# A two-layer transformer with experts: a fourth buffer for split weights, kept rows fetched two at a time, and the last activation's low part ahead of the next expert's rows

## The chip, the cores and the metric

The kernel runs on one core of a Trainium2 chip, as one program. The metric is the device time of one execution in microseconds (us), lower is better. Three executions of the kernel before took 1961.27, 1962.09 and 1963.03 us; the median is 1962.09 us.

## The reference, cut to what matters

The program computes two blocks of two layers each in float32 (sequence 256, width 1024). The change lies in the mixture of experts, the feed-forward part of the first block's second layer:

```python
def swiglu(x, wg, wu, wd):
    return (jax.nn.silu(x @ wg) * (x @ wu)) @ wd

def moe_swiglu(xn, router, wg, wu, wd):       # 8 experts, top 2, inner width 3584
    t = xn.reshape(B * S, D)                  # 256 tokens x 1024
    logits = (t @ router).astype(jnp.float32)
    top_val, top_idx = lax.top_k(logits, TOP_K)
    gates = jax.nn.softmax(top_val, axis=-1)
    combine = jnp.sum(jax.nn.one_hot(top_idx, N_EXPERTS) * gates[..., None], axis=1)
    out = jnp.zeros_like(t)
    for e in range(N_EXPERTS):
        out = out + combine[:, e:e + 1] * swiglu(t, wg[e], wu[e], wd[e])
    return out
```

Before it stand attention, retention and a dense feed-forward part, behind it a gated embedding and the whole second block; the change leaves those as they are.

## The kernel before

**Pieces and products.** All weights stream from HBM in pieces of 128x2048 float32 (1 MB) into seven slots of the tile `raw`. Products keep float32 precision by splitting: for each piece ScalarE (ACT) writes a rounded copy, the high part (`high<-raw`, L1630 in the experts), and VectorE (DVE) writes the rest, the low part (`low<-raw,high`, L2555). TensorE (PE) then multiplies high by high, high by low and low by high (L726, L727, L728). There are `PARTS` = 3 buffers for the two parts; piece k uses buffer k % 3.

**An expert.** The tokens of an expert (at most 128) are gathered as rows, turned, scaled and split into `xg_hi` (ACT, L1637, eight instructions) and `xg_lo` (DVE, L2538, eight). An expert has 42 pieces, numbered by `EXPERT_ORDER`: for j = 0 to 6 two gate pieces, two up pieces and, from j = 1 on, the two down pieces of j - 1; the two down pieces of j = 6 come last. So gate 3 is pieces 16 and 17, up 3 is 18 and 19, down 2 is 20 and 21; up 6 is 36 and 37, down 5 is 38 and 39, down 6 is 40 and 41. Each piece is 12 matmuls of 512 columns. After gate j (and for j = 6 after piece 38) PE turns the hidden activation of the group before (`turn_hidden`, L1149); ACT copies it as `hT_hi` (L1645), DVE makes `hT_lo` (L2566), and the first matmul of that group's down waits for `hT_lo`.

**What sets the order.** No scheduler is at work: each engine's instructions stand in the order in which the code writes them, with waits on semaphores between engines. `expert` exists once for each of the three engines. On ACT and DVE it walks over the 42 pieces; at step q (piece q has been used by PE) it splits piece q + 3, and where q is the second gate piece of a group it then handles the activation: ACT runs `copy(j - 1)` and the silu (L1661), DVE runs `low_hidden(j - 1)`. At the second up piece DVE first multiplies (L2575) and then splits. At up 6's second piece (q = 37) DVE also runs `gathered` for the next expert; at q = 38 it runs `low_hidden(6)`, before the split of that step. Experts 1 to 6 are a loop, expert 0 and expert 7 are written out. In expert 0 DVE also works out where each token's kept rows lie (`kept_places`, after the split of q = 19).

**Kept rows.** Experts 0 to 6 store their outputs to HBM from `scr` (`expert_traffic` on GpSimd, POOL). In expert 7 POOL fetches each token's rows by four indirect DMAs of 128 rows into the tile `kept` (L1941), which lies over `xT_hi` and `xT_lo`, the tiles of the input activations, idle during the experts. DVE adds them to `h` at q = 13, 19, 25 and 31 (`add_kept`, L2649).

Of the kernel before, what the change touches and what calls it, by code (L numbers as in the profile page):

```python
# [76 lines left out]
EXPERT_ORDER = expert_order()  # L77

# [54 lines left out]
def program(nc, io, out, cut=99):  # L133
    ctx = ExitStack()
    with ctx:
# [102 lines left out]
        kept = sb("kept", [P, 2 * NT, D], over="xT_hi")  # L238
# [57 lines left out]
        moe_sems[1].update(turns=14, by_dma=False)  # L296
        moe_sems[0].update(high=high_done, low=low_done, used=pieces_used, landed=landed, ring=(0, RAW))
# [387 lines left out]
        def _(pe):  # L685
# [413 lines left out]
            def expert(e, s, first, is_first, is_last):  # L1099
# [7 lines left out]
                def product(what, j):  # L1107
                    for half in range(2):
# [14 lines left out]
                        if what == "down":  # L1123
                            w = [x[:, k % PARTS, :].rearrange("p (k n) -> p k n", k=2) for x in (high, low)]
                            columns_first = is_last and (j, half) == (GROUPS - 1, 1)
                            for n in range(4):
                                f, c = (n % 2, n // 2) if columns_first else (n // 2, n % 2)
                                ff = 2 * half + f
                                last = exact(bank[4 + c][:, :], [x[:, j % 2, ff * P:(ff + 1) * P] for x in (hT_hi, hT_lo)],
                                             [x[:, f, c * CHUNK:(c + 1) * CHUNK] for x in w],  # L1130
                                             j == 0 and ff == 0, j == GROUPS - 1 and ff == 3)
                                if columns_first and n == 1:
                                    last.then_inc(s["half"], 1)
                        else:
                            w = [x[:, k % PARTS, :].rearrange("p (k n) -> p k n", k=4) for x in (high, low)]
# [281 lines left out]
        def _(act):  # L1417
# [206 lines left out]
            def expert_split(e, s, first, loads0, k):  # L1624
# [16 lines left out]
            def expert(e, s, first, loads0, is_first, is_last, again=False):  # L1641
# [5 lines left out]
                for q, (what, j, half) in enumerate(EXPERT_ORDER):  # L1647
# [34 lines left out]
            def finish(s, first):  # L1682

                if s["by_dma"]:
                    act.wait_ge(outputs_stored, 16 * N_EXPERTS)
# [21 lines left out]
            def all_experts(s, first, loads0, again):  # L1707
                for k in range(0 if again else 1, PARTS):
                    expert_split(0, s, first, loads0, k)
# [128 lines left out]
            for l in range(LAYERS):  # L1838
# [12 lines left out]
                if l == 1:  # L1851
                    expert_split(0, moe_sems[0], moe_first, moe_landed, 0)
# [65 lines left out]
        def _(pool):  # L1918
# [6 lines left out]
            def expert_traffic(s):  # L1925
# [24 lines left out]
        def _(dve):  # L1950
# [601 lines left out]
            def expert_split(e, s, first, k):  # L2552
                at0, slots = s["ring"]
                dve.wait_ge(s["high"], first + PER_EXPERT * e + k + 1)
                dve.tensor_tensor(low[:, k % PARTS, :], raw[:, at0 + k % slots, :], high[:, k % PARTS, :].bitcast(F32),  # L2555
                                  ALU.subtract).then_inc(s["low"], 1)

            def expert(e, s, first, first_slot, is_first, is_last, again=False):
# [10 lines left out]
                for q, (what, j, half) in enumerate(EXPERT_ORDER):  # L2569
# [7 lines left out]
                    if q + PARTS < PER_EXPERT:  # L2577
                        expert_split(e, s, first, q + PARTS)
                    elif not is_last:
                        expert_split(e + 1, s, first, q + PARTS - PER_EXPERT)  # L2580
                    elif not again and q + PARTS < PER_EXPERT + AHEAD:
# [61 lines left out]
            def add_kept(n):  # L2643

                t = n % NT
                dve.wait_ge(kept_in, 16 * 2 * NT)
                if n >= NT:
                    dve.wait_ge(kept_added, n - NT + 1)
                dve.scalar_tensor_tensor(out=h[:, t, :], in0=kept[:, n, :], scalar=kept_gate[:, n:n + 1],  # L2649
                                         in1=h[:, t, :], op0=ALU.mult, op1=ALU.add).then_inc(kept_added, 1)  # L2650

            def finish(s):

                for c in range(2):
                    y_low(s, N_EXPERTS - 1, c).then_inc(s["ylow"], 1)
                if s["by_dma"]:
                    dve.wait_ge(kept_added, 2 * NT)
# [276 lines left out]
```

## Time and profile before

| what | value |
|---|---|
| median of 3 executions | 1962.09 us |
| profiled execution's own time | 1963.61 us |
| its span, first to last instruction | 1961.8 us |
| PE busy (matmuls) | 1915.7 us, 98% |
| DVE busy | 1516.9 us, 77% |
| ACT busy | 1227.8 us, 63% |
| HBM read | 507.56 MB, mean 262 GB/s |
| expert outputs stored | first at 641.8 us, last at 1364.1 us |

The page names the busy time of each engine, the groups of instructions and who waited for whom. The waits are read first, then the timeline of each engine around the places where PE waited; start times are in us from the span's start. A matmul row's duration (0.39 us) is longer than the distance to the next one, since matmuls overlap: PE's pace is read from the starts. A store of an expert's outputs follows the end of that expert; six experts lie between the first and the last, 120.4 us each.

### The profile page before, as it was taken

To read this page: it belongs to the slowest core of one execution; us is meant where nothing else is said; L and a number is where in the kernel's file an instruction comes from. 1 tells how busy PE (TensorE), PEld (TensorE's weight loads), DVE (VectorE), ACT (ScalarE), POOL (GpSimd) and SP (SyncE) were. 2 spreads that over 40 slices of the span, in tenths; PEclk is the share of its full clock that TensorE was granted. 3 is DMA by queue.
4 is the path that set the end of the run, shared out by engine and by line. 5 is a ranking of instruction groups with operands and counts; after the bars stand their busy time and mean duration, and the time that the engine had idled before them with its cause. 6 is when DMAs were issued, how large, how long until landed. Compare 5 with 4: busy or idle time off the path is not lost.

```text
span 1961.8 us, 26828 instructions
## 1 busy us (share of the span) xinstructions
PE 1915.7 (98%) x10275; PEld 1627.7 (83%) x10275; DVE 1516.9 (77%) x1478; ACT 1227.8 (63%) x1332; POOL 29.8 (2%) x28
## 2 busy tenths in 40 slices
PE   8999999999899999999999999999999999999998
PEld 7879998888688888888888888888887788888987
DVE  5675555656798888888888888888997865877586
ACT  4554535555677777777777777777777546354542
POOL 0000000000000000000000000000100000000000
PEclk9999999999999999999999999999999999999999
DMA  7717555431799999999999999999996452345321
GB/s 250 250 47 259 189 177 171 151 129 70 282 373 355 392 371 376 386 352 392 377 364 384 358 385 384 365 381 357 396 378 226 163 168 97 123 159 193 129 94 37
DMA packets 246211, 514.62 MB, mean 262 GB/s; under 512 B 12516, under 2 KB 59240, under 8 KB 246120
## 3 DMA queue, kind: packets, MB, share of 16 engines
q1 hardware_dynamic: 242936, 502.77, 71.0%
q0 software_dynamic: 2896, 10.49, 1.3%
q8 instruction: 62, 1.02, 0.2%
q14 instruction: 29, 0.24, 0.0%
q10 hardware_dynamic: 288, 0.11, 0.0%
HBM read 507.56 MB, written 5.77 MB: 262 GB/s over the span
## 4 chain that ended last, share of the span: by engine, by line
PE 80%; DVE 11%; ACT 4%; issue 2%; SPq 2%; DMA 1%; DVEq 0%; ACTq 0%
PE bank L726 25%; PE bank L728 24%; PE bank L727 24%; DVE low L1958 3%; DVE low L2555 1%; ACT high L1630 1%; PE bank L697 1%; PE bank L1149 1%; PE bank L850 1%; ACT high L1427 1%; SPq L636 1%; SPq L675 1%; DVE xg_lo L2538 1%; DVE at L2765 1%; PE bank L841 1%
## 5 line engine op out<-in xcount | busy, mean ns | idle before, releaser
L2555 DVE TENSOR_TENSOR low<-raw,high 128x2048 fp32r<-128x2048 f32 x336 | 767.7, 2290 | 110.5 <-ACT high L1630 109.8
L1630 ACT ACTIVATE high<-raw 128x2048 fp32r<-128x2048 f32 x336 | 644.4, 1922 | 244.4 <-PE bank L728 243.0
L1958 DVE TENSOR_TENSOR low<-raw,high 128x2048 fp32r<-128x2048 f32 (+1 forms) x138 | 310.4, 2259 | 162.7 <-ACT high L1427 162.3
L1427 ACT ACTIVATE high<-raw 128x2048 fp32r<-128x2048 f32 (+1 forms) x138 | 260.6, 1894 | 164.7 <-PE bank L728 152.2
L726 PE MATMUL bank<-high,xg_hi 128*128 128x512 f32 x896 | 353.8, 395 | 1.5 <-DVE xg_lo L2538 1.0
L728 PE MATMUL bank<-high,xg_lo 128*128 128x512 f32 x896 | 349.5, 390 | 0.0
L727 PE MATMUL bank<-low,xg_hi 128*128 128x512 f32 x896 | 348.9, 389 | 0.0
L726 PE MATMUL bank<-high,xT_hi 128*128 128x512 f32 (+1 forms) x576 | 227.3, 395 | 3.1 <-DVE xT_lo L1980 1.3
L728 PE MATMUL bank<-high,xT_lo 128*128 128x512 f32 (+1 forms) x576 | 221.5, 385 | 0.0
L727 PE MATMUL bank<-low,xT_hi 128*128 128x512 f32 (+1 forms) x576 | 221.0, 384 | 0.0
L726 PE MATMUL bank<-high,hT_hi 128*128 128x512 f32 x536 | 210.3, 392 | 8.3 <-DVE hT_lo L2566 8.3
L727 PE MATMUL bank<-low,hT_hi 128*128 128x512 f32 x536 | 208.8, 390 | 0.0
L728 PE MATMUL bank<-high,hT_lo 128*128 128x512 f32 x536 | 208.7, 389 | 0.0
L726 PEld LDWEIGHTS bank<-high,xg_hi 128*128 128x128 f32 x896 | 168.3, 188 | 36.3 <-issue 1.3
L728 PEld LDWEIGHTS bank<-high,xg_lo 128*128 128x128 f32 x896 | 168.1, 188 | 35.8
L727 PEld LDWEIGHTS bank<-low,xg_hi 128*128 128x128 f32 x896 | 168.5, 188 | 33.5
L726 PE MATMUL bank<-xT_hi,high 128*128 128x256 f32 x672 | 192.4, 286 | 3.4 <-issue 1.8
L727 PE MATMUL bank<-xT_lo,high 128*128 128x256 f32 x672 | 190.9, 284 | 0.0
L728 PE MATMUL bank<-xT_hi,low 128*128 128x256 f32 x672 | 190.8, 284 | 0.0
L726 PEld LDWEIGHTS bank<-xT_hi,high 128*128 128x128 f32 x672 | 129.6, 193 | 4.7 <-issue 2.0
L727 PEld LDWEIGHTS bank<-xT_lo,high 128*128 128x128 f32 x672 | 129.6, 193 | 0.4
L728 PEld LDWEIGHTS bank<-xT_hi,low 128*128 128x128 f32 x672 | 129.6, 193 | 0.0
(346 smaller groups left out, 2208.8 us busy)
## 6 DMA issues: line engine op xcount, KB each, us to landing
raw<-in_moe_w_gate SPq DMA_DIRECT2D x112, 1024.0 KB, 6.9
raw<-in_moe_w_up SPq DMA_DIRECT2D x112, 1024.0 KB, 7.1
raw<-in_moe_w_down SPq DMA_DIRECT2D x112, 1024.0 KB, 7.0
raw<-in_w_in SPq DMA_DIRECT2D x63, 1024.0 KB, 5.1
raw<-in_w_out SPq DMA_DIRECT2D x20, 1024.0 KB, 4.8
raw<-in_dense_w_gate SPq DMA_DIRECT2D x11, 1024.0 KB, 5.2
raw<-in_dense_w_up SPq DMA_DIRECT2D x11, 1024.0 KB, 5.2
raw<-in_dense_w_down SPq DMA_DIRECT2D x11, 1024.0 KB, 4.8
```

The costliest lines, as they stand in the source:

```text
L636: sp.dma_start(dst, src).then_inc(landed[slot], 16)
L675: sp.dma_start(dst, source).then_inc(consts_in, 16)
L697: last = pe.transpose(bank_of(key)[:, (k * NT + t) * P:(k * NT + t + 1) * P], rows[:, t, (2 * j + k) * P:(2 * j + k + 1) * P], ident[:, :])
L726: pe.matmul(dst, stationary[0], moving[0], start=start, stop=False)
L727: pe.matmul(dst, stationary[0], moving[1], start=False, stop=False)
L728: return pe.matmul(dst, stationary[1], moving[0], start=False, stop=stop)
L841: last = pe.transpose(bank[2 + g % 2][:, b * P:(b + 1) * P], probs[:, g % 2, b * P:(b + 1) * P], ident[:, :])
L850: last = pe.matmul(att_out(name, u, t), probsT[:, g % 2, c0 + s * P:c0 + (s + 1) * P], val[:, s, :], start=(s == 0), stop=(s == n // P - 1))
L1427: act.activation(high[:, slot, 0:k * n], raw[:, raw_slot[piece], 0:k * n], ACT.Copy).then_inc(high_done, 1)
L1630: act.activation(high[:, k % PARTS, :], raw[:, slot, :], ACT.Copy).then_inc(s["high"], 1)
L1958: dve.tensor_tensor(low[:, slot, 0:k * n], src, high[:, slot, 0:k * n].bitcast(F32), ALU.subtract).then_inc(low_done, 1)
L2555: dve.tensor_tensor(low[:, k % PARTS, :], raw[:, at0 + k % slots, :], high[:, k % PARTS, :].bitcast(F32), ALU.subtract).then_inc(s["low"], 1)
```

## The change

Four things change.

1. In the experts' main pass split weights get a fourth buffer, `high3` over `xT_hi` and `low3` over `xT_lo`. `expert_parts(4)` gives buffers k % 4 to pieces 0 to 11, three buffers (0, 1, 2) in turn to pieces 12 to 17, and four again to pieces 18 to 41, so that each expert begins at buffer 0. Its list `ahead[q]` says which pieces are split at step q: mostly piece q + 4; at q = 11 none; at q = 12 to 16 piece q + 3; at q = 17 pieces 20 and 21; from q = 18 on piece q + 4 again.
2. `kept` moves to the two tiles `a2` and `scr`: POOL fetches two blocks of rows, and each of the other two only when DVE has added the block that lay in its place.
3. DVE runs `gathered` for the next expert at q = 38, behind `low_hidden(6)`, instead of at q = 37, ahead of it.
4. `finish` waits for the added rows before it reuses `scr` and `a2`.

```diff
+def expert_parts(slots):
+    three = 6 if slots == 4 else len(EXPERT_ORDER)
+    start = 12 if slots == 4 else 0
+    slot = [k % 4 if k < start else ((k - start) % 3 if k < start + three else (k - start - three) % 4)
+            for k in range(len(EXPERT_ORDER))]
+    n = len(slot)
+    prev = [max(i for i in range(-n, k) if slot[i % n] == slot[k]) for k in range(n)]
+    ahead, at = [[] for _ in range(n)], slots
+    for q in range(n):
+        while at < n + slots and (prev[at] if at < n else prev[at - n] + n) <= q:
+            ahead[q].append(at)
+            at += 1
+    return slot, prev, ahead
...
-        kept = sb("kept", [P, 2 * NT, D], over="xT_hi")
+        kept = (a2, scr)
+        high3 = sb("high3", [P, HALF], F32R, over="xT_hi")
+        low3 = sb("low3", [P, HALF], F32R, over="xT_lo")
...
 (ACT, expert_split)
-                act.wait_ge(s["used"], first + PER_EXPERT * e + k - PARTS + 1)
-                act.activation(high[:, k % PARTS, :], raw[:, slot, :], ACT.Copy).then_inc(s["high"], 1)
+                act.wait_ge(s["used"], first + PER_EXPERT * e + s["part_before"][k] + 1 + (s["by_dma"] and is_first and k < PARTS))
+                act.activation(expert_part(s, k)[0], raw[:, slot, :], ACT.Copy).then_inc(s["high"], 1)
...
 (ACT, expert; DVE the same)
-                    if q + PARTS < PER_EXPERT:
-                        expert_split(e, s, first, loads0, q + PARTS)
-                    elif not is_last:
-                        expert_split(e + 1, s, first, loads0, q + PARTS - PER_EXPERT)
-                    elif not again and q + PARTS < PER_EXPERT + AHEAD:
+                    for k in ([PARTS] if is_first and q == 0 and s["by_dma"] else []) + s["parts_ahead"][q]:
+                        if k < PER_EXPERT:
+                            expert_split(e, s, first, loads0, k)
+                        elif not is_last:
+                            expert_split(e + 1, s, first, loads0, k - PER_EXPERT)
+                    if is_last and not again and PER_EXPERT <= q + PARTS < PER_EXPERT + AHEAD:
                         split(moe_first + N_EXPERTS * PER_EXPERT + q + PARTS - PER_EXPERT)
...
 (POOL, expert_traffic)
+                pool.wait_ge(rows_turned, 2 * (N_EXPERTS - 1))
                 pool.wait_ge(outputs_stored, 16 * N_EXPERTS)
                 for n in range(2 * NT):
-                    pool.indirect_dma_start(kept[:, n, :], None, expert_rows,
+                    if n >= 2:
+                        pool.wait_ge(kept_added, n - 1)
+                    pool.indirect_dma_start(kept[n % 2][:, :], None, expert_rows,
...
 (DVE, expert)
+                    if (what, j, half) == ("down", GROUPS - 2, 0) and not is_last and s["by_dma"]:
+                        gathered(rows_high, 2 * e, rows_low, (1, 3))
...
-                    if (what, j, half) == ("up", GROUPS - 1, 1) and not is_last:
-                        if s["by_dma"]:
-                            gathered(rows_high, 2 * e, rows_low, (1, 3))
-                        else:
-                            gathered(s["thigh"], 9 * e + 8, s["tfree"], (7, 6))
+                    if (what, j, half) == ("up", GROUPS - 1, 1) and not is_last and not s["by_dma"]:
+                        gathered(s["thigh"], 9 * e + 8, s["tfree"], (7, 6))
...
 (DVE, add_kept)
-                dve.wait_ge(kept_in, 16 * 2 * NT)
+                dve.wait_ge(kept_in, 16 * 2 * (n // 2 + 1))
```

**First place: DVE in expert 0 around gate 3.** The rows run from the end of up 2 (the product into `v_63` on bank2) to the same product of up 3 (bank3). Before, five splits (pieces 16 to 20) stand between that product and `hT_lo` of group 2:

```order
L2575 TENSOR_TENSOR v_63<-v_63,bank2 128x512 [waits pieces_used,moe0_silu]
L2555 TENSOR_TENSOR low_51<-raw_49,high_50 128x2048 [waits high_parts_done] x5
L2566 TENSOR_TENSOR hT_lo_111<-bank7,hT_hi_110 128x512 [waits moe0_thigh]
L2555 TENSOR_TENSOR low_51<-raw_49,high_50 128x2048 [waits high_parts_done]
L2575 TENSOR_TENSOR v_63<-v_63,bank3 128x512 [waits pieces_used,moe0_silu]
```

After the change, in the same stretch (`low3` is the low half of the fourth buffer):

```order
L2609 TENSOR_TENSOR v_63<-v_63,bank2 128x512 [waits pieces_used,moe0_silu]
L2589 TENSOR_TENSOR low_51<-raw_49,high_50 128x2048 [waits high_parts_done] x5
L2589 TENSOR_TENSOR low3_116<-raw_49,high3_115 128x2048 [waits high_parts_done]
L2600 TENSOR_TENSOR hT_lo_111<-bank7,hT_hi_110 128x512 [waits moe0_thigh]
L2589 TENSOR_TENSOR low_51<-raw_49,high_50 128x2048 [waits high_parts_done]
L2609 TENSOR_TENSOR v_63<-v_63,bank3 128x512 [waits pieces_used,moe0_silu]
```

Six splits (16 to 21) now stand there: step 17 splits pieces 20 and 21, both ahead of `hT_lo` of group 2. On ACT both high parts likewise stand ahead of `hT_hi` of that group.

**Second place: DVE at the end of expert 0.** The rows run from the last multiplication (up 6, into `v_63`) to the last split of the expert's code. Before:

```order
L2575 TENSOR_TENSOR v_63<-v_63,bank2 128x512 [waits pieces_used,moe0_silu]
L2555 TENSOR_TENSOR low_51<-raw_49,high_50 128x2048 [waits high_parts_done]
L2538 SCALAR_TENSOR_TENSOR xg_lo_107<-bank1,gcols_74,xg_hi_106 128x128 [waits taken_rows_high]
L2538 SCALAR_TENSOR_TENSOR xg_lo_107<-bank1,gcols_74,xg_hi_106 128x128 x3
L2538 SCALAR_TENSOR_TENSOR xg_lo_107<-bank3,gcols_74,xg_hi_106 128x128 [waits taken_rows_high]
L2538 SCALAR_TENSOR_TENSOR xg_lo_107<-bank3,gcols_74,xg_hi_106 128x128 x3
L2566 TENSOR_TENSOR hT_lo_111<-bank7,hT_hi_110 128x512 [waits moe0_thigh]
L2555 TENSOR_TENSOR low_51<-raw_49,high_50 128x2048 [waits high_parts_done] x4
```

After:

```order
L2609 TENSOR_TENSOR v_63<-v_63,bank2 128x512 [waits pieces_used,moe0_silu]
L2589 TENSOR_TENSOR low3_116<-raw_49,high3_115 128x2048 [waits high_parts_done]
L2600 TENSOR_TENSOR hT_lo_111<-bank7,hT_hi_110 128x512 [waits moe0_thigh]
L2571 SCALAR_TENSOR_TENSOR xg_lo_107<-bank1,gcols_74,xg_hi_106 128x128 [waits taken_rows_high]
L2571 SCALAR_TENSOR_TENSOR xg_lo_107<-bank1,gcols_74,xg_hi_106 128x128 x3
L2571 SCALAR_TENSOR_TENSOR xg_lo_107<-bank3,gcols_74,xg_hi_106 128x128 [waits taken_rows_high]
L2571 SCALAR_TENSOR_TENSOR xg_lo_107<-bank3,gcols_74,xg_hi_106 128x128 x3
L2589 TENSOR_TENSOR low_51<-raw_49,high_50 128x2048 [waits high_parts_done] x3
L2589 TENSOR_TENSOR low3_116<-raw_49,high3_115 128x2048 [waits high_parts_done]
```

`hT_lo` of group 6 now stands ahead of the eight `xg_lo`, and the split ahead of it is that of piece 41 instead of piece 40.

## Rows read from the trace of the kernel before

**Rows 1.** The page: busy us, share of the span, instructions.
```profile
PE 1915.7 (98%) x10275; PEld 1627.7 (83%) x10275; DVE 1516.9 (77%) x1478; ACT 1227.8 (63%) x1332; POOL 29.8 (2%) x28
```

**Rows 2.** Waits of PE over the span: us in total, times, longest.
```profile
PE bank L726 <- DVE hT_lo L2566: 8.3, 7, 1.3
...
PE bank L726 <- DVE low L2555: 0.4, 1, 0.4
```

**Rows 3.** Timeline of PE, expert 1, piece 39 to 40: start, us, instruction.
```profile
751.57 0.39 PE L728 MATMUL bank<-high,hT_lo 128*128 128x512 f32 x1
753.12 0.50 PE L726 MATMUL bank<-high,hT_hi 128*128 128x512 f32 x1 [1.17 <-DVE hT_lo L2566]
753.46 0.40 PE L727 MATMUL bank<-low,hT_hi 128*128 128x512 f32 x1
```

**Rows 4.** Timeline of ACT, end of expert 1.
```profile
746.08 1.92 ACT L1630 ACTIVATE high<-raw 128x2048 fp32r<-128x2048 f32 x1 [0.80 <-PE bank L728]
747.91 2.15 ACT L1637 ACTIVATE xg_hi<-bank,gcols 128x128 fp32r<-128x128 f32 x8
749.90 0.65 ACT L1645 ACTIVATE hT_hi<-bank 128x512 fp32r<-128x512 f32 x1
```

**Rows 5.** Timeline of DVE, end of expert 1.
```profile
747.52 0.68 DVE L2575 TENSOR_TENSOR v<-v,bank 128x512 f32<-128x512 f32 x1
748.12 2.28 DVE L2555 TENSOR_TENSOR low<-raw,high 128x2048 fp32r<-128x2048 f32 x1
750.32 2.15 DVE L2538 SCALAR_TENSOR_TENSOR xg_lo<-bank,gcols,xg_hi 128x128 fp32r<-128x128 f32 x8
752.39 0.68 DVE L2566 TENSOR_TENSOR hT_lo<-bank,hT_hi 128x512 fp32r<-128x512 f32 x1
```

**Rows 6.** Timeline of PE, expert 0, piece 39 to 40.
```profile
631.03 0.39 PE L728 MATMUL bank<-high,hT_lo 128*128 128x512 f32 x1
632.74 0.47 PE L726 MATMUL bank<-high,hT_hi 128*128 128x512 f32 x1 [1.32 <-DVE hT_lo L2566]
633.04 0.40 PE L727 MATMUL bank<-low,hT_hi 128*128 128x512 f32 x1
```

**Rows 7.** Timeline of PE, expert 0, before piece 23.
```profile
581.25 0.39 PE L728 MATMUL bank<-high,xg_lo 128*128 128x512 f32 x1
582.07 0.50 PE L726 MATMUL bank<-high,xg_hi 128*128 128x512 f32 x1 [0.43 <-DVE low L2555]
```

**Rows 8.** Timeline of PE, expert 0, before piece 5.
```profile
529.28 0.39 PE L728 MATMUL bank<-high,xg_lo 128*128 128x512 f32 x1
529.62 0.50 PE L726 MATMUL bank<-high,xg_hi 128*128 128x512 f32 x1
```

**Rows 9.** Timeline of ACT, expert 2, step 17 (gate 3).
```profile
809.27 1.92 ACT L1630 ACTIVATE high<-raw 128x2048 fp32r<-128x2048 f32 x1 [0.80 <-PE bank L728]
811.10 0.57 ACT L1645 ACTIVATE hT_hi<-bank 128x512 fp32r<-128x512 f32 x1
```

**Rows 10.** Timeline of DVE, expert 2, step 17 (gate 3).
```profile
811.22 2.29 DVE L2555 TENSOR_TENSOR low<-raw,high 128x2048 fp32r<-128x2048 f32 x1 [0.43 <-ACT high L1630]
813.43 0.68 DVE L2566 TENSOR_TENSOR hT_lo<-bank,hT_hi 128x512 fp32r<-128x512 f32 x1
```

**Rows 11.** Timeline of PE, expert 2, last matmuls of piece 19, first of 20.
```profile
812.04 0.39 PE L728 MATMUL bank<-high,xg_lo 128*128 128x512 f32 x1
...
814.76 0.39 PE L728 MATMUL bank<-high,xg_lo 128*128 128x512 f32 x1
814.98 0.39 PE L726 MATMUL bank<-high,hT_hi 128*128 128x512 f32 x1
```

**Rows 12.** Timeline of DVE, expert 7: second and third block added.
```profile
1421.69 1.28 DVE L2649 SCALAR_TENSOR_TENSOR h<-kept,kept_gate,h 128x1024 f32<-128x1024 f32 x1
...
1438.53 1.28 DVE L2649 SCALAR_TENSOR_TENSOR h<-kept,kept_gate,h 128x1024 f32<-128x1024 f32 x1
```

**Rows 13.** The tile `kept`: its four fetches, issue to landing.
```profile
DMA to landing us min/median/max: 8.5/9.1/10.1
```

More of the change, by code:

```diff
@@ L237, in program, with expert_part @@
         taken_rows = a2
-        kept = sb("kept", [P, 2 * NT, D], over="xT_hi")
+        kept = (a2, scr)
+        high3 = sb("high3", [P, HALF], F32R, over="xT_hi")
+        low3 = sb("low3", [P, HALF], F32R, over="xT_lo")
+        def expert_part(s, k):
+            slot = s["part"][k]
+            return (high[:, slot, :], low[:, slot, :]) if slot < PARTS else (high3[:, :], low3[:, :])
         logit_rows = yf[0:N_EXPERTS, NT * D:NT * D + SEQ]
@@ L296, in program @@
         moe_sems[1].update(turns=14, by_dma=False)
+        for s, slots in zip(moe_sems, (PARTS + 1, PARTS)):
+            s["part"], s["part_before"], s["parts_ahead"] = expert_parts(slots)
         moe_sems[0].update(high=high_done, low=low_done, used=pieces_used, landed=landed, ring=(0, RAW))
@@ L1123, in product @@
                         if what == "down":
-                            w = [x[:, k % PARTS, :].rearrange("p (k n) -> p k n", k=2) for x in (high, low)]
+                            w = [x.rearrange("p (k n) -> p k n", k=2) for x in expert_part(s, k)]
                             columns_first = is_last and (j, half) == (GROUPS - 1, 1)
@@ L1134, in product @@
                         else:
-                            w = [x[:, k % PARTS, :].rearrange("p (k n) -> p k n", k=4) for x in (high, low)]
+                            w = [x.rearrange("p (k n) -> p k n", k=4) for x in expert_part(s, k)]
                             dst = bank[(0 if what == "gate" else 2) + j % 2]
@@ L1622, in attention2, with expert_split @@
                 splits(pieces_of["ih", l][1])
-            def expert_split(e, s, first, loads0, k):
+            def expert_split(e, s, first, loads0, k, is_first=False):
                 at0, slots = s["ring"]
@@ L1708, in all_experts @@
                 for k in range(0 if again else 1, PARTS):
-                    expert_split(0, s, first, loads0, k)
+                    expert_split(0, s, first, loads0, k, True)
                 gathered(s["tfull"], 1, s["thigh"], (6, 7))
@@ L2554, in expert_split @@
                 dve.wait_ge(s["high"], first + PER_EXPERT * e + k + 1)
-                dve.tensor_tensor(low[:, k % PARTS, :], raw[:, at0 + k % slots, :], high[:, k % PARTS, :].bitcast(F32),
+                high_part, low_part = expert_part(s, k)
+                dve.tensor_tensor(low_part, raw[:, at0 + k % slots, :], high_part.bitcast(F32),
                                   ALU.subtract).then_inc(s["low"], 1)
@@ L2576, in expert @@
                                           ALU.mult).then_inc(s["hm"], 1)
[L2577 to L2581, printed above, removed]
+                    if (what, j, half) == ("down", GROUPS - 2, 0) and not is_last and s["by_dma"]:
+                        gathered(rows_high, 2 * e, rows_low, (1, 3))
+                    for k in ([PARTS] if is_first and q == 0 and s["by_dma"] else []) + s["parts_ahead"][q]:
+                        if k < PER_EXPERT:
+                            expert_split(e, s, first, k)
+                        elif not is_last:
+                            expert_split(e + 1, s, first, k - PER_EXPERT)
+                    if is_last and not again and PER_EXPERT <= q + PARTS < PER_EXPERT + AHEAD:
                         split(moe_first + N_EXPERTS * PER_EXPERT + q + PARTS - PER_EXPERT)
@@ L2645, in add_kept @@
                 t = n % NT
[L2646 removed]
+                dve.wait_ge(kept_in, 16 * 2 * (n // 2 + 1))
                 if n >= NT:
                     dve.wait_ge(kept_added, n - NT + 1)
[L2649 removed]
+                dve.scalar_tensor_tensor(out=h[:, t, :], in0=kept[n % 2][:, :], scalar=kept_gate[:, n:n + 1],
                                          in1=h[:, t, :], op0=ALU.mult, op1=ALU.add).then_inc(kept_added, 1)
             def finish(s):
+                if s["by_dma"]:
+                    dve.wait_ge(kept_added, 2 * NT)
                 for c in range(2):
                     y_low(s, N_EXPERTS - 1, c).then_inc(s["ylow"], 1)
[L2656 to L2657 removed]
                 for n in range(4):
```

4 lines of the change are left out of this document (2 added, 2 removed).

## The prediction

> **What bounds the kernel now.** I read the busy shares first: PE is busy for 1915.7 of 1961.8 us [rows 1]. So a gain can only come from PE's own waits, and DVE and ACT matter only where PE waits for one of their results. The list of waits comes next. Of those that the change can touch, one is large: PE waits seven times for `hT_lo`, 8.3 us in all, the longest 1.3; for a low part (`low` L2555) it waits once, 0.4 us [rows 2]. Then the timeline of PE shows where: between piece 39 and piece 40 of an expert, once in each of experts 0 to 6 (expert 7 gathers nothing for a next one). PE's undisturbed pace is read from starts: twelve matmuls from 812.04 to 814.76, so 0.227 us each and 2.72 us a piece [rows 11].
>
> A wait costs more than its idle time. In expert 1 the matmul behind 751.57 starts at 753.12: 1.55 us instead of 0.227, so 1.32 lost; the one after it starts 0.34 later instead of 0.227, 0.11 more: 1.43 us [rows 3]. In expert 0: 1.71 less 0.227 is 1.48, then 0.30 instead of 0.227: 1.55 us [rows 6]. Less the largest, the other six have (8.3 - 1.3) / 6 = 1.17 us of idle each, the same as in rows 3, so they repeat. Seven waits cost 1.55 + 6 x 1.43 = 10.1 us. Two small ones in expert 0 are for low parts that come late: before piece 23 0.82 - 0.227 = 0.59, and with the slow restart of rows 3 0.70 us [rows 7]; before piece 5 0.34 - 0.227 = 0.11, with restart 0.22 us [rows 8].
>
> **End of an expert: DVE reordered, one more buffer.** Take expert 1. PE's end of piece 37 releases ACT at 746.08 [rows 4]. That step now splits piece 41 instead of 40; its duration and trigger are those of the row. ACT then makes `xg_hi` from 747.91 and `hT_hi` from 749.90 to 750.55, as before. DVE multiplies at 747.52 and splits from 748.12 to 750.40 [rows 5]. Before, the eight `xg_lo` (2.15 us) stood next and `hT_lo` ended at 753.07. Now `hT_lo` is next, waits for 750.55 and ends at about 751.26. PE wants it at 751.57 + 0.23 = 751.80, so it is there 0.54 us early. The `xg_lo` then end at about 753.4 and the low part of the next expert's piece 0 at about 755.6 (2.2 us after). PE wants both two pieces later, at 751.80 + 5.44 = 757.24: 1.6 us of cover. Each half of the change alone would not do: with three buffers piece 41's low part would follow the `xg_lo` and end at about 755.6 against a need at 754.5. All seven waits go, -10.1 us.
>
> The fourth buffer gives every other split outside the three-buffer stretch one piece, 2.72 us, more lead than its trigger gives it now. The lateness of 0.59 and 0.11 us in expert 0 is less than that: -0.9 us. If it stays after all, this term is 0.
>
> **Step 17: two splits ahead of one activation.** This is what speaks against the change. The return from three buffers to four needs one step that splits two pieces, and it is step 17, the second gate piece of group 3, which also carries the activation of group 2. The order shows six splits instead of five ahead of that `hT_lo`. In expert 2 the stretch now reads: ACT splits from 809.27 and copies `hT_hi` from 811.10 [rows 9]; DVE splits from 811.22 and makes `hT_lo` from 813.43, so it ends at 814.11 [rows 10]; PE wants it at 814.98 [rows 11]. Cover: 0.87 us. After the change ACT splits piece 20 at 809.27, piece 21 one step later (1.83 us, from rows 9) at 811.10 to 813.02, and copies `hT_hi` at 812.93 to 813.5. DVE splits piece 20 at 811.22, piece 21 at 811.22 + 2.20 (the step from 748.12 to 750.32 in rows 5) = 813.42, and `hT_lo` runs 2.21 later (rows 10), at 815.63 to 816.31. PE starts 0.05 behind (753.07 to 753.12 in rows 3 and 5), at 816.36 instead of 814.98: 1.38 us, with the restart 1.49. Nothing hides it: piece 20 is the first to read that activation, and PE has no other work in its program in between. The landing of piece 21's weights is not in question, since its split is asked for only one step early.
>
> It happens in all eight experts, since all run with four buffers: 8 x 1.49 = +11.9 us. No row shows two splits ahead of a small copy at this place, so I bound it: 0.87 us of cover against one DVE split of 2.20 to 2.29 gives 1.33 to 1.42; with a restart of 0.07 to 0.11 that is 1.4 to 1.5, and if ACT or DVE fall a further 0.2 behind, 1.7; if something I do not see lets DVE begin 0.3 us sooner, 1.1. So +8.8 to +13.6, and I take 11.9. Behind it DVE and ACT are one piece ahead, and piece 22 onward has its low part in time.
>
> The engine's order is what this term hangs on. In the trace DVE did not take `hT_lo` ahead of the `xg_lo` written before it, although its input was there at 750.55 and it ran at 752.39 [rows 4, 5]. The Trainium skill (Perfetto Trace Analysis, Tensor Engine Instruction) says that ScalarE, VectorE and GpSimd queues are strict FIFO and only TensorE's has a limited reorder, for weight loads; by that rule the term stands, by an engine that picked the ready instruction it would be 0. The trace agrees with the rule.
>
> **Kept rows in pairs.** The third and fourth fetch start only after an add. The fourth may start when the second add is over, 1421.69 + 1.28 = 1422.97 [rows 12]; the longest of four landings took 10.1 us [rows 13], so by 1433.1. The third add, which waits for that pair, stands at 1438.53 [rows 12]. Cover: 5.4 us, and PE another 2.7 behind DVE's. The queue holds nothing else then. Cost 0; were a landing 10 us later than any seen, +2 us. The first pair is fetched as now: the added wait, for rows turned in expert 6, is over by then. In `finish` the changed wait is for adds that ended 20 us before.
>
> **New tiles.** Splits into `low3` and `high3` have the same shape. No row shows them; for a duration as of the nearest rows, 0; a few per cent either way would vanish in the lead of 2.7 us.
>
> **The sum.** -10.1 - 0.9 + 11.9 = +0.9 us. The span goes from 1961.8 to 1962.7, the profiled execution's own time from 1963.61 to 1964.5. The three timed runs lie 1.5 us lower than that execution, at a median of 1962.09: predicted 1962.9 us. I call within 0.2% (3.9 us: 1958.2 to 1966.0) no change; it is about what a measurement of this kernel can tell.
>
> **The rivals.**
> - *The second split at step 17 hides.* Only the end-of-expert waits and the two small ones go: 1962.1 - 11.0 = 1951.1 us. For it: DVE idles before most splits, 0.43 us in rows 10, and the step before (q = 11 without a split) leaves it free. Against it: that idle lies before the first of the two splits, which still waits for PE's release; and 2.2 us is more than the cover of 0.87. 0.11.
> - *The end-of-expert wait stays, and the new one comes on top: slower.* Place: `hT_lo` of group 6. It holds only if it ends before 751.80, and its input comes from ACT at 750.55, behind `xg_hi`. If ACT's part slides by more than 0.54 us, the wait is back in part; if it slides by 1.8 us, all of it. Price: 10.1 us not saved, so -0.9 + 11.9 = +11.0, 1973.1 us. For it: the cover is the thinnest of all. Against it: ACT's four instructions and their triggers are unchanged in kind and count. 0.07.
> - *The fetch of kept rows comes too late*: +2 us at 10 us late, inside my range. 0.03.
>
> **How the numbers follow.** The forecast has 0.79. Its own bounds are -11.0 or -10.1, with +8.8 to +13.6: -2.2 to +3.5, so 1959.9 to 1965.6 us. The range reaches a little to both sides for a wait half removed or half as long, 1958.5 to 1967.0; that leaves out the fast and the slow rival, 0.18. Faster 0.12 (the fast rival and a little), same 0.78, slower 0.10 (the slow rival, and a new wait longer than bounded).
>
> **What would show it.** The changed profile should have no PE wait for `hT_lo` between pieces 39 and 40, and eight between pieces 19 and 20, each about 1.2 us of idle, 120 us apart; the total of waits for `hT_lo` would go from 8.3 to about 10. No PE wait for a low part in the experts. Outputs stored 120.4 us apart, as now. The fourth fetch lands before 1434 and the third add follows its split without a gap. I am wrong if the wait at piece 20 is missing or under 0.5 us, or if waits at piece 40 remain.

## The result, and the profile after

| | before | changed |
|---|---|---|
| median of 8 runs, us | 1962.12 (1961.27 to 1963.11) | 1967.79 (1966.16 to 1972.19) |
| profiled execution, us (its span) | 1963.61 (1961.8) | 1967.32 (1965.5) |

The ratio is 1.0023 with the 95% interval 1.0014 to 1.0031. On the 1962.09 us of the start that is 1966.6 us; the forecast was 1962.9 in a range that ends at 1967.0. So the change costs 2.7 to 6.1 us where no change was forecast. The middle of that interval, 4.5 us, is above the 3.9 us that I called no change, and its lower end is below. The same kernel measured once more (experiment 10) gave 1.0026 (1.0015 to 1.0037), so the loss is real and about 4.5 to 5 us.

The page, to be read beside [rows 1]: PE's work is unchanged, the span is 3.7 us longer.

```profile
span 1965.5 us, 26840 instructions
...
PE 1916.3 (97%) x10275; PEld 1629.0 (83%) x10275; DVE 1515.1 (77%) x1478; ACT 1226.1 (62%) x1332; POOL 31.0 (2%) x28
```

The lines of the changed kernel are numbered some 30 higher: L755 to L757 are the old L726 to L728, the low split is L2589, `hT_lo` L2600, `xg_lo` L2571, `select`'s probabilities L2558, the kept add L2683. The waits of PE in the experts (us in total, times, longest), beside [rows 2]:

```profile
PE bank L755 <- DVE hT_lo L2600: 10.1, 8, 1.4
...
PE bank L755 <- DVE xg_lo L2571: 2.1, 1, 2.1
...
PE bank L1196 <- DVE probs L2558: 1.7, 1, 1.7
```

The wait for a low part in the experts is gone. `hT_lo` has eight waits where it had seven, and they are at another place. The wait for `xg_lo` stands ahead of expert 0's first piece and was 1.0 us; it is taken up with the sum below. End of expert 1, DVE, beside [rows 5] (start, us, instruction, in brackets the idle time ahead of it and what ended it):

```profile
751.43 2.29 DVE L2589 TENSOR_TENSOR low<-raw,high 128x2048 fp32r<-128x2048 f32 x1
753.90 0.69 DVE L2600 TENSOR_TENSOR hT_lo<-bank,hT_hi 128x512 fp32r<-128x512 f32 x1 [0.18 <-ACT hT_hi L1674]
754.51 2.15 DVE L2571 SCALAR_TENSOR_TENSOR xg_lo<-bank,gcols,xg_hi 128x128 fp32r<-128x128 f32 x8
```

and PE at the same place, beside [rows 3]:

```profile
754.89 0.39 PE L757 MATMUL bank<-high,hT_lo 128*128 128x512 f32 x1
755.11 0.39 PE L755 MATMUL bank<-high,hT_hi 128*128 128x512 f32 x1
```

`hT_lo` ends at 754.59 and piece 40 begins at 755.11 without a gap: 0.52 us of cover, 0.54 predicted. Step 17 in expert 2, first ACT, then DVE, then PE, beside [rows 9 to 11]:

```profile
811.13 3.72 ACT L1659 ACTIVATE high<-raw 128x2048 fp32r<-128x2048 f32 x2 [0.80 <-PE bank L757]
814.76 0.58 ACT L1674 ACTIVATE hT_hi<-bank 128x512 fp32r<-128x512 f32 x1
```

```profile
813.09 4.49 DVE L2589 TENSOR_TENSOR low<-raw,high 128x2048 fp32r<-128x2048 f32 x2 [0.43 <-ACT high L1659]
817.50 0.68 DVE L2600 TENSOR_TENSOR hT_lo<-bank,hT_hi 128x512 fp32r<-128x512 f32 x1
```

```profile
816.62 0.39 PE L757 MATMUL bank<-high,xg_lo 128*128 128x512 f32 x1
818.24 0.50 PE L755 MATMUL bank<-high,hT_hi 128*128 128x512 f32 x1 [1.23 <-DVE hT_lo L2600]
818.57 0.39 PE L756 MATMUL bank<-low,hT_hi 128*128 128x512 f32 x1
```

`hT_hi` was ready at 815.34, and DVE was busy with the second low split until 817.58. PE starts 1.62 us after 816.62 instead of 0.227, so 1.39 lost, and the next matmul 0.33 later instead of 0.227: 1.50 us. It stands in all eight experts (575.57, 696.15, 816.62 and so on to 1419.20). In the first and the last of them the step from start to start is 1.77 us, so these two cost 1.62 us each and the eight together 12.2.

What the forecast did not have is in expert 0, at the token matmul behind piece 5. PE of the kernel before:

```profile
532.26 0.39 PE L728 MATMUL bank<-high,xg_lo 128*128 128x512 f32 x1
533.32 0.58 PE L1167 MATMUL bank<-a,probs 128*128 128x1 f32 x4 [0.67 <-DVE probs L2525]
...
534.46 0.39 PE L727 MATMUL bank<-low,xg_hi 128*128 128x512 f32 x1
534.69 0.40 PE L728 MATMUL bank<-high,xg_lo 128*128 128x512 f32 x1
```

and of the changed kernel:

```profile
532.16 0.39 PE L757 MATMUL bank<-high,xg_lo 128*128 128x512 f32 x1
534.24 0.58 PE L1196 MATMUL bank<-a,probs 128*128 128x1 f32 x4 [1.69 <-DVE probs L2558]
...
536.57 0.63 PE L756 MATMUL bank<-low,xg_hi 128*128 128x512 f32 x1
537.00 0.63 PE L757 MATMUL bank<-high,xg_lo 128*128 128x512 f32 x1
```

From start to start the gap is 2.08 us instead of 1.06, so 1.0 more. Behind it the matmuls of piece 6 start 0.43 us apart instead of 0.23. The stretches by window (us, busy time of PE, PEld, DVE, ACT and POOL, granted clock, DMA share, GB/s), before and after:

```profile
533.00:540.00 7.00, 6.68 (x34) 5.70 (x35) 6.20 (x7) 4.57 (x5) 1.04 (x1) 1.00 1.02 361
```

```profile
533.00:540.00 7.00, 5.76 (x23) 4.78 (x24) 6.26 (x10) 2.91 (x4) 0.41 (x1) 0.76 0.99 363
```

In this stretch the granted clock, 1.00 (2.4 GHz) before, was at 0.5 (1.2 GHz) for 3.4 us from 535.5 on. Piece 6 took 4.40 us instead of 2.85: 1.55 us more. Why `probs` comes later is seen on DVE. Before:

```profile
530.09 2.28 DVE L2555 TENSOR_TENSOR low<-raw,high 128x2048 fp32r<-128x2048 f32 x1
532.29 0.16 DVE L2522 COPY ssum<-routing 128x2 f32<-128x2 f32 x1
```

After:

```profile
520.87 6.70 DVE L2589 TENSOR_TENSOR low<-raw,high 128x2048 fp32r<-128x2048 f32 x3 [2.80 <-ACT high L1659]
...
531.00 2.29 DVE L2589 TENSOR_TENSOR low<-raw,high 128x2048 fp32r<-128x2048 f32 x1
533.21 0.16 DVE L2555 COPY ssum<-routing 128x2 f32<-128x2 f32 x1
```

With a fourth buffer expert 0 splits four pieces instead of three ahead. That extra split stands ahead of `select` (the picking of the next expert's tokens, at step 3), and `select` starts 0.92 us later.

The sum over the experts, as differences of PE's gaps: -10.2 (seven waits) - 0.9 (before pieces 23 and 5, both gone) + 12.2 (eight waits) + 1.0 (token matmul) + 1.6 (half clock) = +3.7 us. It is to be held against the experts alone, from the first matmul of expert 0 to the last one of expert 7 that reads `hT_lo`. Before:

```profile
508.19 6.48 PE L1222 MATMUL bank<-probs,yf 128*128 128x128 f32 x32 [0.65 <-DVE probs L2525]
...
515.81 0.47 PE L726 MATMUL bank<-high,xg_hi 128*128 128x512 f32 x1 [1.03 <-DVE xg_lo L2538]
...
1478.80 0.39 PE L728 MATMUL bank<-high,hT_lo 128*128 128x512 f32 x1
```

After:

```profile
508.59 5.23 PE L1251 MATMUL bank<-probs,yf 128*128 128x128 f32 x32 [0.87 <-DVE probs L2558]
...
515.98 0.47 PE L755 MATMUL bank<-high,xg_hi 128*128 128x512 f32 x1 [2.06 <-DVE xg_lo L2571]
...
1482.61 0.39 PE L757 MATMUL bank<-high,hT_lo 128*128 128x512 f32 x1
```

That is 962.99 us before and 966.63 after, +3.64. PE waits 1.0 us longer for `xg_lo` here, but the 32 small matmuls ahead of it took 1.25 us less, and expert 0 starts only 0.17 us later. That the whole spans also differ by 3.7 us is therefore partly chance. In the second profile of the changed kernel (experiment 10) the experts take 966.58 us, the same, but they start at 513.20 and the span is 1962.0 us, hardly more than before.

### The profile page after: what moved, and what is told of

It is laid out like the page before. It is cut to its first block, busy times and chain, and to the rows that moved or that the text cites. A ratio compares the mean times of both kernels' runs of the same rounds, so it can differ in the third digit from the quotient of the medians.

```text
span 1965.5 us, 26840 instructions
## 1 busy us (share of the span) xinstructions
PE 1916.3 (97%) x10275; PEld 1629.0 (83%) x10275; DVE 1515.1 (77%) x1478; ACT 1226.1 (62%) x1332; POOL 31.0 (2%) x28
## 4 chain that ended last, share of the span: by engine, by line
PE 83%; DVE 9%; ACT 4%; issue 3%; DMA 0%; ACTq 0%; DVEq 0%
PE bank L755 26%; PE bank L757 25%; PE bank L756 25%; DVE low L1991 3%; PE bank L726 1%; ACT high L1659 1%; PE bank L1178 1%; ACT high L1456 1%; PE bank L879 1%; DVE low L2589 1%; DVE at L2799 1%; PE bank L870 1%; PE bank L848 1%; DVE kT L2824 0%; DVE qT L2823 0%
## 5 line engine op out<-in xcount | busy, mean ns | idle before, releaser
L2589 DVE TENSOR_TENSOR low<-raw,high 128x2048 fp32r<-128x2048 f32 x336 | 765.5, 2290 | 110.9 <-ACT high L1659 109.3
L755 PE MATMUL bank<-high,xg_hi 128*128 128x512 f32 x896 | 354.0, 395 | 2.1 <-DVE xg_lo L2571 2.1
L757 PE MATMUL bank<-high,xg_lo 128*128 128x512 f32 x896 | 350.1, 391 | 0.0
L755 PE MATMUL bank<-high,xT_hi 128*128 128x512 f32 (+1 forms) x576 | 227.2, 394 | 3.4 <-DVE xT_lo L2013 1.3
L757 PE MATMUL bank<-high,xT_lo 128*128 128x512 f32 (+1 forms) x576 | 221.4, 384 | 0.0
L755 PE MATMUL bank<-high,hT_hi 128*128 128x512 f32 x536 | 210.4, 392 | 10.1 <-DVE hT_lo L2600 10.1
L757 PE MATMUL bank<-high,hT_lo 128*128 128x512 f32 x536 | 208.7, 389 | 0.0
L755 PEld LDWEIGHTS bank<-high,xg_hi 128*128 128x128 f32 x896 | 168.7, 188 | 35.9 <-issue 2.3
L757 PEld LDWEIGHTS bank<-high,xg_lo 128*128 128x128 f32 x896 | 168.5, 188 | 35.9
L755 PE MATMUL bank<-xT_hi,high 128*128 128x256 f32 x672 | 193.0, 287 | 3.7 <-issue 2.1
L757 PE MATMUL bank<-xT_hi,low 128*128 128x256 f32 x672 | 191.2, 284 | 0.0
L755 PEld LDWEIGHTS bank<-xT_hi,high 128*128 128x128 f32 x672 | 130.1, 194 | 5.2 <-issue 2.4
L757 PEld LDWEIGHTS bank<-xT_hi,low 128*128 128x128 f32 x672 | 130.1, 194 | 0.0
```

Of the source, the lines that this page charges most:

```text
L755: pe.matmul(dst, stationary[0], moving[0], start=start, stop=False)
L757: return pe.matmul(dst, stationary[1], moving[0], start=False, stop=stop)
L2589: dve.tensor_tensor(low_part, raw[:, at0 + k % slots, :], high_part.bitcast(F32), ALU.subtract).then_inc(s["low"], 1)
```

## The experiments

Each is a variant of the changed kernel. Ratios are to the kernel before, run beside it on the same chip, with their 95% intervals. Before had a median of 1963.54 us beside the first four, 1963.32 beside the next four and 1961.91 beside the last two. Where a stretch of the experts is given, it runs between the two matmuls named above. My theory: the double step at 17 costs 12 us, the lead in expert 0 ahead of `select` some 2.6 to 4, and all the rest is free. The rivals: the kept rows in pairs or the new buffers themselves cost something; the 1.0023 is scatter.

**1. The double step later.** One number moves the three-buffer stretch to pieces 20 to 25 and the double step from 17 to 25.

```diff
-    start = 12 if slots == 4 else 0
+    start = 20 if slots == 4 else 0
```

> Only the place of the three-buffer stretch moves: pieces 20 to 25 instead of 12 to 17, so that the step that splits two pieces is 25 (second piece of up 4), where no activation is copied. My theory (two splits ahead of one activation): the eight PE waits for hT_lo between pieces 19 and 20 go, 8 x 1.5 = 12 us, no others come, and the time is 1967.8 - 12 = about 1956 us, 0.3% below the kernel before. Rival (any step with two splits costs the same, wherever it stands): eight waits of 1.4 us move to pieces 26 or 28 and the time stays at 1967 to 1968. Rival (the loss is in memory or clock, not in this wait): under 3 us of change.

Measured: 1954.0 us (1952.28 to 1954.66), ratio 0.9953 (0.9939 to 0.9966). The list of waits:

```profile
PE bank L1196 <- DVE probs L2558: 1.8, 1, 1.8
PE bank L755 <- DVE xg_lo L2571: 1.1, 1, 1.1
PE bank L755 <- DVE hT_lo L2600: 0.6, 1, 0.6
```

Fifteen of the waits in question are gone, old and new; one of 0.6 us is left, in expert 7, where four splits stand between a kept add and that `hT_lo`. The place of the double step is the difference between loss and gain: 0.70% or 14 us against the changed kernel. In the profiles the experts take 953.54 us instead of 966.63, 13.1 less: 12.2 for the eight waits and 1.6 because the clock does not fall behind the token wait, less 1.0 for that last wait and a slightly longer token wait, make 12.8.

**2. `select` ahead of step 3's splits.** It stood behind them.

```diff
+                    if (what, j, half) == ("up", 0, 1) and not is_last and s["by_dma"]:
+                        select(e + 1, s, first_slot, e + 1)
...
-                    if (what, j, half) == ("up", 0 if s["by_dma"] else 2, 1) and not is_last:
+                    if (what, j, half) == ("up", 2, 1) and not is_last and not s["by_dma"]:
```

> DVE picks the next expert's tokens (select, four small instructions) ahead of the split of step 3 instead of behind it; all else as in the changed kernel. My theory for what the forecast left out: in expert 0 the extra early split pushes select back by 0.93 us, PE's wait at piece 6 grows from 0.83 to 1.85 us, and the clock that falls behind it costs another 1.6 us. Then this wait goes in expert 0 (the pick is done 2.2 us earlier), the eight matmuls at half clock go, and the time falls by 1.85 + 1.6 = 3.5 us plus 6 x 0.2, to about 1963; the scatter of the runs (6 us) falls to that of the kernel before (2 us). Rival (the clock falls there by chance, whatever PE did): the wait goes but some stretch at half clock stays in or near expert 0, and the scatter stays at 6 us; about 1965.5.

Measured: 1964.51 us (1961.09 to 1966.28), ratio 1.0004 (0.9995 to 1.0013). DVE now has `probs` before the splits, and `hT_lo` behind them:

```profile
530.09 0.48 DVE L2558 TENSOR_SCALAR probs<-a,ssum 128x128 f32<-128x128 f32 x2
...
530.69 6.70 DVE L2589 TENSOR_TENSOR low<-raw,high 128x2048 fp32r<-128x2048 f32 x3
...
537.37 0.68 DVE L2600 TENSOR_TENSOR hT_lo<-bank,hT_hi 128x512 fp32r<-128x512 f32 x1
```

The token matmul no longer waits and the clock is not lowered behind it, but a ninth wait for `hT_lo` appears (0.6 us idle, 0.8 lost, at 537; list: 10.8 us, 9 times). The experts take 963.70 us, 2.9 less than in the changed kernel; by the ratios it is 0.19 to 0.22% off the changed kernel's 1.0023 and 1.0026, some 4 us. The expected smaller scatter did not come: the runs lie 5 us apart, and those of the kernel before lie 8 us apart on this chip.

**3. Both.** The two edits above together.

```diff
-    start = 12 if slots == 4 else 0
+    start = 20 if slots == 4 else 0
...
+                        select(e + 1, s, first_slot, e + 1)
```

> The two edits before together: double step at 25, select ahead of the split. My theory: both savings add, 1967.8 - 12 - 4.7 = about 1951 us. Rival (one wait hides the other's saving): above 1954.

Measured: 1953.08 us (1951.76 to 1954.28), ratio 0.9950 (0.9937 to 0.9964). The waits:

```profile
PE bank L755 <- DVE hT_lo L2600: 1.2, 2, 0.6
```

This lies between the 1951 us of the expectation and the 1954 of its rival. It is 0.03% better than the first and not 0.2%: within the intervals the second edit adds little here. In the profiles the experts take 952.12 us instead of 953.54, 1.4 less: the token wait (2.0 us) goes and a wait for `hT_lo` at piece 8 comes (0.8 us lost). The first's profile already had no lowered clock behind its token wait, so in it there was less to gain; that is a reading of one execution each, not a proof.

**4. The second split of step 17 behind the activation.** The places in the buffers stay, only the order in the step changes, on ACT and DVE alike.

```diff
-                    for k in (...) + s["parts_ahead"][q]:
+                    for k in (...) + (s["parts_ahead"][q][:1] if q == 17 else s["parts_ahead"][q]):
...
+                        for k in s["parts_ahead"][q][1:] if q == 17 else ():
+                            expert_split(e, s, first, k)
```

> Step 17 stays the double step, but ACT and DVE split piece 21 behind the activation of group 2 instead of ahead of it. My theory: hT_lo then ends at the same point as in the kernel before, all eight waits at piece 20 go, 1967.8 - 12 = about 1956 us, the same as with the stretch moved. Rival (two splits in a step are too much work for DVE at that place, in whatever order): the wait turns up at piece 21 or 22 as a late low part and half or more of the 12 us stays.

Measured: 1957.2 us (1952.96 to 1959.83), ratio 0.9966 (0.9953 to 0.9979). DVE in expert 2, where `hT_lo` follows one split:

```profile
809.06 2.29 DVE L2591 TENSOR_TENSOR low<-raw,high 128x2048 fp32r<-128x2048 f32 x1 [0.43 <-ACT high L1659]
811.27 0.68 DVE L2602 TENSOR_TENSOR hT_lo<-bank,hT_hi 128x512 fp32r<-128x512 f32 x1
811.87 4.48 DVE L2591 TENSOR_TENSOR low<-raw,high 128x2048 fp32r<-128x2048 f32 x2
```

The eight waits at piece 20 go with the order alone: it was the place in DVE's program, not the buffers. Three shorter waits are left elsewhere (1.5 us), and the token matmul waits 2.4 us with a half clock behind it. The last of the three follows an add of kept rows for which DVE waited, in this experiment alone:

```profile
1431.46 1.28 DVE L2687 SCALAR_TENSOR_TENSOR h<-a,kept_gate,h 128x1024 f32<-128x1024 f32 x1 [1.83 <-DMA scr<-expert_rows,kept_row]
```

So the kept rows in pairs are free in the changed kernel and not in each variant of it; the last section comes back to this.

**5. The lead built later.** Expert 0 keeps three pieces of lead to step 3 and takes its fourth at step 4, behind `select`.

```diff
+                    early = is_first and s["by_dma"]
-                    for k in (...) + s["parts_ahead"][q]:
+                    for k in [q + 3] if early and q < 4 else ([7, 8] if early and q == 4 else s["parts_ahead"][q]):
```

> As the changed kernel, but expert 0 keeps three pieces of lead up to step 3 and gains the fourth at step 4, behind select: the extra split no longer stands ahead of select. My theory (the extra split delays select and with it PE at piece 6): the wait at piece 6 is back at 0.8 us as in the kernel before, 1.0 us less than in the changed one, and the clock behind it falls less often; ratio to the kernel before about 1.000 to 1.001 instead of 1.0023. The eight waits at piece 20 stay. Rival (the start of expert 0 has nothing to do with it): the wait at piece 6 stays at 1.8 us.

Measured: 1964.19 us (1962.27 to 1968.67), ratio 1.0006 (0.9998 to 1.0015). As in the second experiment, by another edit: no token wait, no lowered clock there, a ninth wait for `hT_lo`. The expectation was 0.8 us of token wait, as in the kernel before; it went altogether. The splits of steps 1 to 3 write a buffer that PE gave back one piece earlier, and behind the first silu ACT makes the next four high parts without a pause (from 524.01), where it made two in the kernel before and then waited for PE.

```profile
PE bank L755 <- DVE hT_lo L2601: 11.1, 9, 1.4
```

Two different edits, with only the order of `select` and the extra split in common, both take some 3 to 4 us off, though the intervals of 1.0006 and 1.0023 still touch (1.0014 to 1.0015) and the two do not come from one measurement. The profiles show the mechanism in both; here the experts take 964.37 us, 2.3 less than in the changed kernel.

**6. Four buffers, `gathered` at its old step 37.**

```diff
-                    if (what, j, half) == ("down", GROUPS - 2, 0) and not is_last and s["by_dma"]:
-                        gathered(rows_high, 2 * e, rows_low, (1, 3))
...
+                    if (what, j, half) == ("up", GROUPS - 1, 1) and not is_last:
+                        if s["by_dma"]:
+                            gathered(rows_high, 2 * e, rows_low, (1, 3))
```

> Fourth buffer and pairs as in the changed kernel, but DVE makes xg_lo at step 37, ahead of the low part of the last activation, as before. My theory (the order of DVE alone removes the wait at piece 40, the fourth buffer removes the one that would follow it): both sets of waits stand, eight at piece 20 and seven at piece 40 of 1.3 to 1.5 us, the time is that of the changed kernel plus 10 us, ratio about 1.0075. Rival (one more piece of lead alone removes the wait): no wait at piece 40, ratio 1.002.

Measured: 1976.74 us (1975.87 to 1979.65), ratio 1.0072 (1.0058 to 1.0087).

```profile
PE bank L755 <- DVE hT_lo L2600: 18.5, 15, 1.4
```

Eight new waits and all seven old ones; the token matmul waits 2.4 us, with a half clock behind it. A fourth buffer without the new order removes none.

**7. Three buffers with the new order.**

```diff
-        for s, slots in zip(moe_sems, (PARTS + 1, PARTS)):
+        for s, slots in zip(moe_sems, (PARTS, PARTS)):
```

> Three buffers as before, no double step, but DVE makes xg_lo behind the last activation's low part, and kept rows in pairs. My theory: the wait moves from piece 40 (for hT_lo) to piece 41 (for its low part, which now follows xg_lo) and stays about 1.2 us, seven times; ratio 0.998 to 1.000. Rival (the reorder alone is what gains): no wait in its place, ratio 0.995, as with the double step moved.

Measured: 1960.99 us (1958.98 to 1963.96), ratio 0.9992 (0.9983 to 1.0001). DVE, then PE, at the end of expert 1:

```profile
749.52 2.15 DVE L2571 SCALAR_TENSOR_TENSOR xg_lo<-bank,gcols,xg_hi 128x128 fp32r<-128x128 f32 x8
751.59 6.68 DVE L2589 TENSOR_TENSOR low<-raw,high 128x2048 fp32r<-128x2048 f32 x3
```

```profile
752.62 0.39 PE L757 MATMUL bank<-high,hT_lo 128*128 128x512 f32 x1
753.93 0.50 PE L755 MATMUL bank<-high,hT_hi 128*128 128x512 f32 x1 [0.92 <-DVE low L2589]
```

The wait moves one piece on, from `hT_lo` at piece 40 to piece 41's low part, and is 0.92 instead of 1.17 us. So each half of the change alone is worth next to nothing, as the forecast had it (1.1 us late by its times, 1.08 measured: 1.31 - 0.227).

**8. Three buffers, old order, kept rows in pairs.** Both undone; only `kept` over `a2` and `scr`, fetched two at a time, is left.

```diff
-        for s, slots in zip(moe_sems, (PARTS + 1, PARTS)):
+        for s, slots in zip(moe_sems, (PARTS, PARTS)):
...
-                    if (what, j, half) == ("down", GROUPS - 2, 0) and not is_last and s["by_dma"]:
-                        gathered(rows_high, 2 * e, rows_low, (1, 3))
```

> Only the kept rows in pairs; three buffers, DVE's old order. My theory: no cost and no gain, ratio 1.000 within 0.001; the fourth fetch lands before the third add is due, 5 us early. Rival (part of the 4 us that the forecast missed is a late fetch in expert 7): DVE waits at the third add and the ratio is 1.001 or more.

Measured: 1962.81 us (1961.2 to 1966.45), ratio 0.9997 (0.9988 to 1.0006). The pairs cost nothing that the interval can show.

**9. The best of all.** The double step at 25, `select` first, and in expert 0 three pieces of lead to step 5, the fourth at step 6.

```diff
-    start = 12 if slots == 4 else 0
+    start = 20 if slots == 4 else 0
...
+                        select(e + 1, s, first_slot, e + 1)
+                    early = is_first and s["by_dma"]
+                    for k in [q + 3] if early and q < 6 else ([9, 10] if early and q == 6 else s["parts_ahead"][q]):
```

> Double step at 25, select ahead of the split, and in expert 0 three pieces of lead up to step 5, the fourth gained at step 6. From the changed kernel: -11.9 (eight waits at piece 20), -1.9 (the wait at piece 6), -1.6 on average or less (half clock behind it), 6 x 0.2 (the pick in the other experts), and none of the 0.8 us at piece 8 that the version with both edits shows. My theory: ratio to the kernel before 0.9945 to 0.9950, about 1953 us beside a kernel before of 1963.5. Rival (the lead given up at the start is missed elsewhere in expert 0): a new wait for a low part there and a ratio no better than 0.9950.

Measured: 1952.94 us (1950.01 to 1955.24), ratio 0.9948 (0.9934 to 0.9962): it beats both kernels, and cannot be told from the first and third experiments. What PE still waits for in the experts:

```profile
PE bank L755 <- DVE xg_lo L2572: 2.9, 1, 2.9
...
PE bank L755 <- DVE hT_lo L2601: 0.6, 1, 0.6
```

No wait is left at pieces 6 and 8. The wait ahead of expert 0's first piece is longer here (2.9 us; 2.1 in the changed kernel, 1.0 in the kernel before), and the clock fell to half behind it.

**10. The changed kernel once more**, without an edit.

> The changed kernel once more, so that it stands beside the others and the kernel before on one chip. Theory (it is slower by the extra wait of 1 us at piece 6, by the half clock that often follows it, and by 0.9 us net of the moved waits): ratio 1.0015 to 1.0030. Rival (the first measurement owed 3 us to its chip): ratio 1.0005 or less.

Measured: 1967.12 us (1963.9 to 1969.15), ratio 1.0026 (1.0015 to 1.0037). Its profile repeats the token wait (1.7 us), the eight waits (10.1 us) and the lowered clock (0.79 from 533 to 540). The profiled execution is the fastest of the seven (1963.9 us), although the experts cost the same 3.6 us in it: they start 2.6 us earlier than in the profile of the kernel before.

## Why the prediction was right, and where not

**Seven waits at the end of an expert, -10.1 us.** Right in place, count and size: none is left at piece 40, with 0.52 us of cover (0.54 predicted). The claim that both halves are needed held (experiments 6 and 7).

**Two late low parts in expert 0, -0.9 us.** Right by themselves: the 0.70 before piece 23 and the 0.22 before piece 5 are both gone. But this is the step that failed: "The fourth buffer gives every other split outside the three-buffer stretch one piece, 2.72 us, more lead" counts the lead as a gain alone. A lead has to be built, and in expert 0 it is built by one more split of 2.29 us on a DVE whose program holds `select` at step 3, behind it. PE already waited for `select`'s result in the kernel before (0.67 us, no cover at all). That wait stood in the list from which [rows 2] come (`PE bank L1167 <- DVE probs L2525: 0.7, 1, 0.7`); I left it out of those that the change can touch and did not follow what else stood behind the added split. Counted as the other steps were, from 532.29 and 533.21, it gives about +1.0 us. The lowered clock behind it, +1.6 in the profile, could not be foreseen from the profile before: its wait at this place is followed by the full clock.

**Step 17, +11.9 us.** Right: eight waits, six of them with 1.39 us of lost time and 0.11 of restart, 1.50 against 1.49, and two of 1.62 (experts 0 and 7), 12.2 us in all. DVE kept to its program's order with `hT_hi` ready for 2.2 us (the rows of 813.09 to 817.50, beside [rows 9, 10]). Experiments 1 and 4 take the wait away by two other means.

**Kept rows in pairs, 0; new tiles, 0.** Right for this kernel. Experiment 8 gives 0.9997, and the low splits take 2.28 to 2.30 us each in both profiles. POOL issues the fourth fetch at 1427.29, when the second add is over, and the third add follows its split without idle time:

```profile
1440.17 2.28 DVE L2589 TENSOR_TENSOR low<-raw,high 128x2048 fp32r<-128x2048 f32 x1
1442.37 1.28 DVE L2683 SCALAR_TENSOR_TENSOR h<-a,kept_gate,h 128x1024 f32<-128x1024 f32 x1
```

But the cover was smaller than the 5.4 us of the forecast, and the sign "lands before 1434" did not come true. The slowest of the four landings took 11.8 us, so it ended by 1439.1 at the latest, 3.3 us ahead of the add. In experiment 4 the cover was used up.

The pace of the experts shows no other cost either: from one expert to the next the distance to the kernel before grows by only 0.07 us (+1.50 and -1.43).

**The sum.** +0.9 was forecast, +3.6 stands in the experts of both profiles, +2.7 to +6.1 in the runs. The term left out explains +2.6 of it. The middle values of the runs, 4.5 and 5.1 us, are 1 to 1.5 us above the profiles, and that is open: among the twelve profiles the start of expert 0 moves by up to 4 us, and single runs of one kernel lie 2 to 8 us apart.

That 1966.6 us still falls in the range is in part luck. The range reached up to 1967.0 for waits that the forecast had and might have mis-sized. Those came out as sized; what filled the room was a term that it did not have.

## What to carry to other kernels

Another buffer is worth what its lead covers, less what building and giving back the lead costs: each place where two units of work stand in one step delayed all that was behind them on ACT and DVE, and the start is such a place as well as the return. Look there for small results that PE waits for already; the wait with no cover passed on the whole delay (0.92 us on DVE, 1.0 on PE). Then look at where the double step is placed: here one number (12 to 20) turned +0.23% into -0.47%.

## What the hardware showed that I had not expected

The granted clock fell to half for 3.4 us in the middle of a kernel in which PE is busy 97% of the time, just behind a PE wait. A gap here is the time from one matmul's start to the next one's. Of the five profiles with a gap of 2.1 to 2.8 us at the token matmul, four show it (the changed kernel twice, experiments 4 and 6), experiment 1 with 2.23 us does not; with a gap of 1.06 us (before, experiments 7 and 8) none does. So a wait of 1 us more cost 2.6, and it doesn't do so each time. The eight gaps of 1.6 to 1.8 us at piece 20 are followed by the full clock in every profile that has them. Nor is this the only such stretch. From 505 to 515, ahead of expert 0, where PE runs small matmuls between waits of up to 2.2 us, the clock was at 0.66 on average in the kernel before and at 0.83 in the changed kernel; the 32 small matmuls took 6.48 and 5.23 us. Such stretches are a likely reason why the start of expert 0 moves; that was not tested.

POOL's issue of an indirect DMA of the same size took 0.98, 2.46, 2.74 and 4.94 us in the profile of the changed kernel; nothing waited for it there. For the fourth fetch its length goes with what DVE does beside it: 0.93 or 0.94 us in experiments 1, 3 and 9, where DVE is idle for some 1.35 us; 2.74 in experiment 7, beside two low splits without a pause; 4.94 in the changed kernel, beside three; 9.35 in experiment 4, beside four. There the landing took 15.9 us, and this is the fetch that DVE waited 1.83 us for. No experiment varied this alone, so the cause is not shown.
